# One 128-column stationary block in four, the rest as two 64-column halves: the gate and up products of the first expert layer

## The reference, cut to what matters

```python
def ec_moe(h, w_router, w_e_gate, w_e_up, w_e_down):
    b, t, d = h.shape
    cap = EC_CAPACITY * t // N_EXPERTS          # 64 of 512 latent, 32 of 256 context tokens
    aff = softmax(h @ w_router)
    vals, idx = lax.top_k(swapaxes(aff, 1, 2), cap)
    xs = h[idx]                                 # the rows that each expert chose
    hid = silu(xs @ w_e_gate) * (xs @ w_e_up)   # 1024 -> 1408, twice
    ys = (hid @ w_e_down) * vals                # 1408 -> 1024
    return zeros.at[idx].add(ys)
```

## Time and profile before

| | |
|---|---|
| time, three runs | 3595.4, 3599.0, 3610.7 us; median 3599.0 |
| the profiled execution's own time | 3597.7 us, span 3595.9 us |
| TensorE matmul busy | 94% of the span |
| TensorE weight load busy | 65% |
| VectorE, ScalarE, GpSimd busy | 33%, 20%, 3% |
| mean granted clock of TensorE | 0.989 of full |
| L1308, the line that is changed | 11264 matmuls, busy 486.4 us |

### The profile page before, as it was taken

One profiled execution on the slowest core, in us unless ns is written; L12 is line 12 of the kernel. 1 busy time (PEld: TensorE's weight loads), 2 busy tenths in 40 slices (PEclk: granted clock), 3 DMA queues, 4 the chain that ended last, 5 costly groups with the idle time before them and its releaser, 6 DMA issues.

```text
span 3595.9 us, 74576 instructions
## 1 busy us (share of the span) xinstructions
PE 3397.3 (94%) x32464; PEld 2343.4 (65%) x32464; DVE 1170.0 (33%) x2535; ACT 707.2 (20%) x1346; POOL 99.8 (3%) x171
## 2 busy tenths in 40 slices
PE   7899999999999999999999989899999999999998
PEld 4456757678764777777677656667677565555554
DVE  1443415336624211111111362415265242222222
ACT  3313321122322000000001432321132201111111
POOL 0000100000000000000000000100000000000000
PEclk9999999999999999999999999999999999999999
DMA  5512120020034999999999501220211269999995
GB/s 219 221 51 71 35 82 12 30 71 34 27 129 200 352 367 356 362 366 375 347 358 345 185 31 44 70 82 13 82 45 53 110 262 420 423 419 418 420 421 244
DMA packets 104784, 732.84 MB, mean 204 GB/s; under 512 B 8464, under 2 KB 14864, under 8 KB 61472
## 3 DMA queue, kind: packets, MB, share of 16 engines
q1 hardware_dynamic: 95120, 692.54, 48.7%
q0 software_dynamic: 9360, 35.71, 3.5%
HBM read 706.15 MB, written 16.83 MB: 201 GB/s over the span
## 4 chain that ended last, share of the span: by engine, by line
PE 78%; DMA 9%; DVE 7%; ACT 3%; issue 3%; DVEq 0%; POOL 0%; ACTq 0%; SPq 0%; POOLq 0%
PE psum L709 14%; PE psum L1308 10%; PE psum L1299 8%; PE psum L1337 8%; PE psum L599 8%; PE psum L592 5%; PE psum L1162 4%; PE psum L711 3%; DMA ring<-in_w_e_gate 3%; DMA ring<-in_w_ada 2%; DMA ring<-in_w_e_down 2%; PE psum L1343 2%; PE psum L1353 2%; PE psum L576 2%; DVE work L2045 2%
## 5 line engine op out<-in xcount | busy, mean ns | idle before, releaser
L709 PE MATMUL psum<-HT,ring 128*128 128x256 f32 x2560 | 599.3, 388 | 13.9 <-DVEq L2298 5.3
L709 PEld LDWEIGHTS psum<-HT,ring 128*128 128x128 f32 x2560 | 487.7, 194 | 97.8 <-issue 21.3
L1308 PE MATMUL psum<-work,ring 128*64 128x96 f32 x11264 | 486.4, 248 | 42.5 <-issue 33.1
L1308 PEld LDWEIGHTS psum<-work,ring 128*64 128x64 f32 x11264 | 473.0, 138 | 59.7 <-issue 49.7
L1528 ACT ACTIVATE work<-psum,small 128x768 f32<-128x768 f32 (+4 forms) x208 | 146.1, 703 | 682.7 <-PE psum L1343 323.1
L599 PE MATMUL psum<-ring,HT 128*128 128x512 f32 (+1 forms) x768 | 276.0, 521 | 0.0
L1337 PE MATMUL psum<-ring,work 128*64 128x512 f32 x1056 | 240.6, 597 | 6.4 <-DMA ring<-in_w_e_down 6.3
L1531 ACT ACTIVATE work<-psum 128x256 f32<-128x256 f32 (+7 forms) x219 | 103.5, 473 | 696.1 <-PE psum L1322 259.1
L599 PEld LDWEIGHTS psum<-ring,HT 128*128 128x128 f32 x768 | 145.8, 190 | 127.3 <-issue 120.5
L592 PE MATMUL psum<-HT,ring 128*128 128x256 f32 (+3 forms) x624 | 192.8, 470 | 0.3 <-issue 0.3
L1299 PE MATMUL psum<-ring,work 128*64 128x256 f32 x768 | 173.7, 381 | 0.0
(11 more groups left out here) (249 smaller groups left out, 4021.0 us busy)
## 6 DMA issues: line engine op xcount, KB each, us to landing
ring<-in_w_e_gate SPq DMA_DIRECT2D x48, 2048.0 KB, 10.8
ring<-in_w_e_up SPq DMA_DIRECT2D x48, 2048.0 KB, 11.4
ring<-in_w_e_down SPq DMA_DIRECT2D x48, 2048.0 KB, 10.2
ring<-in_w_ada SPq DMA_DIRECT2D x24, 2048.0 KB, 12.7
ring<-in_w_e_gate SPq DMA_DIRECT2D x24, 1536.0 KB, 9.4
ring<-in_w_e_up SPq DMA_DIRECT2D x24, 1536.0 KB, 9.6
ring<-in_w_e_down SPq DMA_DIRECT2D x24, 1536.0 KB, 10.2
ring<-in_w_gate SPq DMA_DIRECT2D x16, 2048.0 KB, 8.8
```

The source lines that it names most:

```text
L709: pe.matmul(b[:, 0:256], w[:, k, d4 * P:(d4 + 1) * P], HT[:, k, off:off + 256], start=(k == 0), stop=(k == KD - 1))
L1308: ins = pe.matmul(b[lo:lo + 64, f * cap:(f + 1) * cap], w[k][:, c0:c0 + 64], e_xs[:, k, 0:cap], start=(k == 0), stop=(k == KD - 1))
```

## The change

In the first layer's gate and up products, the row blocks k = 3 and k = 7 of each column block use all 128 columns of the weights as one stationary block, in one matmul that writes PSUM partitions 0 to 127. The row blocks k = 0, 1, 2, 4, 5 and 6 stay as two 64-column halves. The order of k, the PSUM addresses, the weights and the semaphores stay.

```diff
                                 b = banks[(0, 2, 0)[g] + u]
                                 for k in range(KD):
-                                    for half in range(2):
-                                        lo, c0 = 64 * half, f * P + 64 * half
-                                        ins = pe.matmul(b[lo:lo + 64, f * cap:(f + 1) * cap], w[k][:, c0:c0 + 64], e_xs[:, k, 0:cap],
-                                                        start=(k == 0), stop=(k == KD - 1))
+                                    cols = 128 if k % 4 == 3 else 64
+                                    for lo in range(0, P, cols):
+                                        ins = pe.matmul(b[lo:lo + cols, f * cap:(f + 1) * cap], w[k][:, f * P + lo:f * P + lo + cols],
+                                                        e_xs[:, k, 0:cap], start=(k == 0), stop=(k == KD - 1))
                             ins.then_inc(sems["gu"], 1)
```

## The result

The changed kernel takes 3789.5 us (median; 3787.6 to 3795.7), the kernel before on the same chip 3597.2: ratio 1.0536, 95% interval 1.0518 to 1.0554, some 192 us more. The forecast was 3812 in a range from 3778 to 3860.

What follows compares the result with a forecast made beforehand. TensorE's single queue was taken to bound the first layer's experts; 257.5 us for width changes less 43 us of waits, 214.5 us, on 3597.7 gave 3812 us, range 3778 to 3860.

Steps and rivals of the forecast that it cites:

- What bounds the stage: First layer's 16 experts, 790.3 us: TensorE bounds, matmuls busy 739.0 us; transfers follow it, and it sometimes runs out of instructions.
- The price of a block: Each full-width block in gate and up costs 372 ns more: 620 ns against 247.5 for the same stretch before.
- Into full width: First full matmul after halves lasts some 350 ns, starts 70 early, ends 280 ns after the last half.
- The second: Second full matmul of a block ends 110 ns after the first, held by its weight load; lower bound 82.5.
- Back: Return to halves: next half starts 70 ns early, lasts 0.30 us, ends 230 ns after the last full matmul.
- Sum of the prediction: Price of all 704 blocks: 689 x 0.372 + 15 x 0.078 = 257.5 us.
- What comes back: TensorE waits saved in the stage: 31 of 34.9 us for instructions, 12 of 14.5 for weights, 43 us.
- bound of 49.4: Most that could come back in the stage: all listed TensorE waits for instructions and weights, 49.4 us.
- a second full matmul at 82.5 ns: Stream rate as lower bound in each block: price 238 us; with 49.4 us back, forecast's low end 3786.
- Hidden loads: Rival, 5%: weight loads run ahead at width changes, so a block costs 187 ns more; 3687 us.
- No pause: Rival, 4%: width changes in gate and up cost nothing, fewer late packets give about -4 us; 3593 to 3598.
- The clock: Rival, 5%: pauses let the granted clock fall in one stretch of four, 110 us on top; 3925 us.

Runs made afterwards that it cites:

- e3: Kernel before with all row blocks of the first layer's gate and up at full width, 128 columns: 3695.6 us, ratio 1.0260.
- e6: Changed kernel, but each weight piece from the first layer's second expert on brings only its first eighth: 3793.4 us, 1.0543 of the kernel before.
- e5: Kernel before, but each weight piece from the first layer's second expert on brings only its first eighth: 3530.9 us, ratio 0.9813.
- e4: Kernel before with row blocks k = 3 and 7 as four 32-column quarters, no full-width matmul: 3736.3 us, ratio 1.0373.
- e12: Kernel before with first-layer down reordered so pieces begin at the width where the last ended, and an eighth of each weight piece from the second expert: 3523.4 us.
- e1: Changed kernel with full-width row blocks at k = 6 and 7 in place of 3 and 7: 3676.4 us, 1.0207 of the kernel before.
- e2: Changed kernel with only row block k = 7 at full width, half as many full blocks: 3665.0 us, 1.0175 of the kernel before.
- e7: Kernel before with whole column blocks f = 3 of the four-column-block pieces at full width, all eight row blocks: 3600.2 us, ratio 1.0003.

## Why the prediction was right, point by point

*What bounds the stage.* Right: TensorE's one queue. All of the change's price arrived in the time, less the waits.

*The price of a block.* Right in each term. Into full width 280 ns: the first full matmul lasts 0.35 us. The second 110 ns later: 112 here and in the long run of e3, so its load sets it, not the stream. Back 230 ns: 0.30 us, started 0.07 early. Sum of the prediction 257.5 us, measured 257.1 by the stages of e6 and e5, 260.1 by their busy times; 689 x (625 - 247.5) ns are 260 too. That the first pair agrees to 0.4 us is luck, since rows read to 10 ns leave 7 us open. Shown by runs, not argued: e3 for the load, e4 and e12 for the change itself, e1 and e2 for the count of changes.

*What comes back.* The mechanism was right, the size was not: 43 us in the sum, with a bound of 49.4. Measured, it is the price less the growth of the stage, 260 - 194 = 66 us, past the bound. This, less the 3 us by which the price was over the sum, is why the stage grew by 194 us and not by 214.5, and why the time fell 22 us under the forecast. That it stayed in the range is in part luck: with the price as forecast and all 49.4 us back the sum gives 3806, more than was measured; the range went lower only because it allowed for a second full matmul at 82.5 ns, which didn't come. The bound was the sum of the idle times that the profile lists. But behind such a wait the array has to fill again. In the kernel before (timeline):

```profile
1314.17 0.55 PE L1308 MATMUL psum<-work,ring 128*64 128x96 f32 x8 [0.34 <-DMA ring<-in_w_e_gate]
1316.24 0.39 PE L1308 MATMUL psum<-work,ring 128*64 128x96 f32 x4 [1.52 <-issue]
```

The one run ends at 1314.72; behind 1.52 us of idle time the next pair starts at 1316.24. It needs 0.25 us to its end and 0.05 for its load, where in the stream a pair ends 0.08 behind the pair ahead: some 0.21 us lost beyond the idle time (0.22 unrounded, at nearly every wait ahead of L1308). The earlier trace rows count 62 such waits, one of them, 0.8 us, behind the end of the stage: 62 x 0.21 = 13 us. Two falls of the clock in the stage cost some 3 us more: in 3.40 us 46 matmuls and 44 in a stretch like it at 1953.7 us (granted clock 0.50 and 0.51), where 82 would stream. These 16 us are what the busy time of the same matmuls shows, 738.4 us against 722.1 in e5; with the idle time that went, 50.6 - 0.8 us, they make the 66.

*The rivals.* Hidden loads: in each of the 672 blocks the first matmul lasts 0.35 us into full width and 0.30 back; not so. No pause: not so. This rival asked whether line and bank make the pauses in the trace before. They don't: from L1308 to L1255 line and bank change and the width, 64, stays.

```profile
1300.08 0.28 PE L1308 MATMUL psum<-work,ring 128*64 128x96 f32 x2
1300.16 0.52 PE L1255 MATMUL psum<-X 128*64 128x2 f32 x13
```

L1255 starts 0.20 us before the end at 1300.36, as in a stream. What I overlooked is that the number of rows can count as the width does: from L962 (64 rows) to L709 (128), both 128 columns wide, the start is 0.07 us before the end (median of 18), while from L606 (128 rows) to L844 (96) it is 0.16, as in a stream (median of 36). The clock: 1.00 in the stage, although matmuls stream for less of it; the two falls of the kernel before, each behind a wait of TensorE (1.71 and 3.37 us), went with the waits.

## What to carry to other kernels

Count the changes of stationary width, not the instructions: each cost 0.13 to 0.2 us here, for the array's emptying and one exposed load. So a mixture costs least in long runs of one width (e7 against the changed kernel), and a piece that begins at the width at which the last one ended saves a change (e12). Price waits that a slower or faster stream will take or give by their idle time and the refill of the array, 0.2 us each here. Before two narrow matmuls are made one wide one, look whether its load holds it back: here two halves of 64 columns came at 82.5 ns a pair, one of 128 at 112.

## What I had not expected of the hardware

The kernel before loses some 43 us of its 3597 to late instructions in this stage (an estimate: 34.9 us in 37 waits, and 0.21 us of refill at each). A run of 128 matmuls with their loads, 256 instructions in 5.5 us, is what one 16 KB packet brings, and beside weight traffic at 359 GB/s the next one came up to 3.4 us late, beside 83 GB/s it was late four times, by up to 1.4 us. Slowing the consumer a little in a few places (e7) removed nearly all of it at the same traffic.
